# Two attention phases of a decoder run as one, over keys and queries that the projection has already split

## The reference

```python
s = einsum('bqhmd,bkhmd->bhmqk', qs, ks) * 64 ** -0.5    # two score maps
s = s + bias(q_pos - k_pos)[h]                           # constant from a distance of 128 on
s = where(q_pos >= k_pos, s, min)
p = softmax(s)
a = p[:, :, 0] - lam * p[:, :, 1]
out = einsum('bhqk,bkhd->bqhd', a, v)
```

## Time and profile before

| | |
|---|---|
| time, median of 3 runs | 3974.72 us (3974.5 to 3978.87) |
| the profiled execution's own time | 3976.59 us |
| its span | 3974.9 us |
| mean granted clock of PE | 0.951 |
| PE / DVE / ACT busy | 3534.9 / 1820.2 / 1157.0 us (89 / 46 / 29% of the span) |
| projections: vg, qka, qk, vg2 | 400, 230, 403, 406 us |
| prompt's attention, then samples' attention | 900, 263 us |

### The profile page before, as it was taken

The page is one execution under the profiler, slowest core; times in us unless marked ns, Lnnn a source line. Parts: engine busy times, 40 slices in busy tenths (PEclk is TensorE's granted clock), DMA queues, the critical chain, the costliest instruction groups (busy, mean ns, idle before and its releaser), DMA issues. The chain is left out here.

```text
span 3974.9 us, 56724 instructions
## 1 busy us (share of the span) xinstructions
PE 3534.9 (89%) x19647; PEld 2921.5 (73%) x19647; DVE 1820.2 (46%) x4012; ACT 1157.0 (29%) x1916; POOL 118.9 (3%) x157
## 2 busy tenths in 40 slices
PE   4999898996899989999999968888988867579999
PEld 3888797674688867887788857777777745468887
DVE  2222211555555532111322168888888822255554
ACT  2111111332221212100211146666666622221111
POOL 0000001110000000000000000000000000000000
PEclk9999998998899999999999979999999988789999
DMA  4211322335322213211412162222121066532221
GB/s 145 74 69 66 108 85 101 101 111 175 127 84 90 73 58 143 74 66 58 159 68 72 58 139 61 60 65 54 44 63 34 12 261 270 222 138 84 78 84 45
DMA packets 305099, 385.40 MB, mean 97 GB/s; under 512 B 153317, under 2 KB 211462, under 8 KB 304918
## 3 DMA queue, kind: packets, MB, share of 16 engines
q1 hardware_dynamic: 304918, 383.18, 29.1%
HBM read 278.63 MB, written 104.47 MB: 96 GB/s over the span
## 5 line engine op out<-in xcount | busy, mean ns | idle before, releaser
L234 PE MATMUL vg_ps_y<-vg_w_hi,vg_x_hi 128*128 128x512 f32 x1088 | 428.3, 394 | 11.1 <-DVE vg_w_lo L307 11.1
L236 PE MATMUL vg_ps_y<-vg_w_lo,vg_x_hi 128*128 128x512 f32 x1088 | 425.1, 391 | 0.0
L238 PE MATMUL vg_ps_y<-vg_w_hi,vg_x_lo 128*128 128x512 f32 x1088 | 425.0, 391 | 0.0
L1506 PE MATMUL att_ps_o<-att_v,att_a_t 128*128 128x128 f32 x2176 | 297.3, 285 | 51.6 <-ACT att_a_t L1567 51.2
L1506 PEld LDWEIGHTS att_ps_o<-att_v,att_a_t 128*128 128x128 f32 x2176 | 279.1, 198 | 76.4 <-ACT att_a_t L1567 53.4
L1634 DVE TENSOR_SCALAR_CACHE_REDUCE att_s<-att_ps_s,att_far 128x512 f32<-128x512 f32 (+3 forms) x608 | 326.5, 581 | 6.0 <-PE att_ps_s L1479 2.2
L1555 ACT ACTIVATE att_s<-att_s,att_neg 128x128 f32<-128x128 f32 (+15 forms) x256 | 307.2, 1200 | 2.3 <-DVE att_neg L1651 1.7
L1478 PE MATMUL att_ps_s<-att_k_hi,att_q_hl 128*128 128x512 f32 (+3 forms) x640 | 262.3, 416 | 11.7 <-DVE att_s L1634 10.8
L234 PEld LDWEIGHTS vg_ps_y<-vg_w_hi,vg_x_hi 128*128 128x128 f32 x1088 | 205.4, 189 | 54.1 <-issue 12.3
L1479 PE MATMUL att_ps_s<-att_k_lo,att_q_hl 128*128 128x512 f32 (+3 forms) x640 | 237.0, 375 | 0.0
L238 PEld LDWEIGHTS vg_ps_y<-vg_w_hi,vg_x_lo 128*128 128x128 f32 x1088 | 205.3, 189 | 42.9
(11 more groups left out here) (270 smaller groups left out, 6103.7 us busy)
## 6 DMA issues: line engine op xcount, KB each, us to landing
smp_k_pg<-in_cache_k SPq DMA_DIRECT2D x64, 512.0 KB, 5.7
smp_v_pg<-in_cache_v SPq DMA_DIRECT2D x64, 512.0 KB
factors<-vg_out SPq DMA_DIRECT2D x68, 256.0 KB, 2.0
res_factors<-factors SPq DMA_DIRECT2D x34, 512.0 KB
res_o<-mixer_out SPq DMA_DIRECT2D x34, 512.0 KB, 4.3
att_k_nat<-out_k SPq DMA_DIRECT2D x128, 128.0 KB, 2.6
att_q_nat<-diff_q SPq DMA_DIRECT2D x128, 128.0 KB, 3.0
gla_x<-gla_qka SPq DMA_DIRECT2D x17, 520.0 KB, 3.4
```

Source lines behind the costliest of these rows:

```text
L234: nc.tensor.matmul(ps_y[g][:, 0:width[g]], x_hi[u][:, k, :], w_hi[:, k, cols], start=(k == 0), stop=False)
L236: nc.tensor.matmul(ps_y[g][:, 0:width[g]], x_hi[u][:, k, :], w_lo[:, k, cols], start=False, stop=False)
L238: mm = nc.tensor.matmul(ps_y[g][:, 0:width[g]], x_lo[u][:, k, :], w_hi[:, k, cols], start=False, stop=(k == KD - 1))
L1506: mm = nc.tensor.matmul(ps_o[:, 0:D_VD], a_t[n % 2][:, (b % 4) * P:(b % 4 + 1) * P], v_sb[u][:, b, :], start=(b == 0), stop=(b == i))
```

## The change

**One projection phase per layer.** `project` now keeps the split x of all 17 tiles resident and streams the weights in pieces of 128 x 512 through a ring of nine, with the groups of columns outside and the tiles inside. It is called once per layer ("gla_in", 7 groups, and "diff_in", 8 groups). The four groups of queries and keys have the kind "turn": PE turns each prompt tile's result (4 transposes, `turn_out`), ACT makes the high part (with the factor 64 ** -0.5 for queries), DVE the low part, and SP stores both, already turned, in `qt`, `kh` and `kl` (5 transfers of 768 KB in all for a tile of queries, 2 of 512 KB for one of keys).

**One attention phase.** `attention` runs sample b beside head h = b. Keys and queries are loaded turned and split, so the `prep`s are gone. Scores go into two buffers of two banks (1024 columns) each: `cut` makes one entry of a tile with n up to 512 (both maps in one buffer), two up to 1024, four above (per map the left part and the right 1024). The low product contracts 64 rows (that map's half of the low keys) in place of 128. DVE takes an entry with one instruction: bias added and sign turned, with a running minimum, and no reduction or negation behind it. Within step g, PE does the first two entries of the scores of step g+2, then what `beside(g)` has of the sample (a key page's 8 transposes at the tiles i = 2 to 5 and 7 to 10; weights and values at i = 14, 15 and at i = 3 of the next head), and then the remaining entries between `turn` and `meet`. The sample's scores use one more entry of the same two buffers at two tiles of each head.

The diff, cut to its core:

```diff
 def project(...):
-        HALF = KD // 2
-        STAGES = 4
-        stage = [sb(f"stage{i}", [P, HALF, BANK]) for i in range(STAGES)]
...
+        x_hi = [sb(f"x_hi{t}", [P, KD, P], F32R) for t in range(TILES)]
+        x_lo = [sb(f"x_lo{t}", [P, KD, P], F32R) for t in range(TILES)]
+        w_hi = [sb(f"w_hi{r}", [P, BANK], F32R) for r in range(RING)]
+        w_lo = [sb(f"w_lo{r}", [P, BANK], F32R) for r in range(RING)]
+        stage = [sb(f"stage{i}", [P, BANK]) for i in range(STAGES)]
...
+                def turn_out(g, t):
+                    n, m = g * TILES + t, turned_before(g, t)
+                    pe.wait_ge(out_done[n % BANKS], after(n // BANKS + 1))
...
+                    for b in range(HB):
+                        mm = nc.tensor.transpose(ps_t[m % 2][:, b * P:(b + 1) * P],
+                                                 out[n % BANKS][:, b * P:(b + 1) * P], core.ident[:, :])
+                    mm.then_inc(s["out_turned"], 1)
...
 def attention(...):
+    def cut(n):
+
+        if n <= BANK:
+            return [[(m, 0, n, m * BANK, m) for m in range(2)]]
+        if n <= WIDE:
+            return [[(m, 0, n, 0, m)] for m in range(2)]
+        return [[(m, lo_, hi_, 0, m)] for m in range(2) for lo_, hi_ in ((0, n - WIDE), (n - WIDE, n))]
...
+                            for first, last, off in pieces:
+                                nc.tensor.matmul(dst[:, off:off + last - first], qs[:, m, :],
+                                                 k_hi[u][m][:, first:last], start=True, stop=False)
+                            half = slice(m * D_DH, (m + 1) * D_DH)
+                            for first, last, off in pieces:
+                                mm = nc.tensor.matmul(dst[:, off:off + last - first], qs[half, 2, :],
+                                                      k_lo[u][half, first:last], start=False, stop=True)
...
+                for g in range(STEPS):
+                    ahead = scores(g + 2) if g + 2 < STEPS else iter(())
+                    for _ in range(SLOTS):
+                        next(ahead, None)
+                    beside(g)
+                    mixed = values(g)
+                    for _ in ahead:
+                        next(mixed, None)
+                    for _ in mixed:
+                        pass
...
+                            nc.vector.tensor_tensor_reduce(
+                                out=sc[g % 2][:, m, lo_:hi_], in0=ps_s[(before + c) % SLOTS][:, off:off + w],
+                                in1=bias[h % 2][:, edge - w:edge], scale=-1.0,
+                                scalar=neg[g % 2][:, m, 0:1] if chained else 3.0e38, op0=ALU.add, op1=ALU.min,
+                                accum_out=neg[g % 2][:, m, side:side + 1]).then_inc(s["taken"], 1)
...
 def decoder(...):
-        project(core, "qka", x, w_gla[0], [
+        project(core, "gla_in", x, w_gla[0], halves(2 * GK, "copy", v)
+                + halves(2 * GK + GV, "silu", factors, g_gla[0]) + [
...
-        project(core, "qk", x1, w_diff[0], halves(0, "copy", q2) + halves(D, "copy", k_out))
+        project(core, "diff_in", x1, w_diff[0], halves(2 * D, "copy", v_out)
...
-        attention(core, q2, k_out, v_out, rev, rel_bias, o2)
-        core.end_phase()
-        sample_attention(core, q2, k_out, v_out, cache_k[0], cache_v[0], table, rev, rel_bias, o2)
+        attention(core, qt, kh, kl, q2, k_out, v_out, cache_k[0], cache_v[0], table, rev, rel_bias, o2)
```

More of the change, by code:

```diff
@@ L155, in project, with ps @@
[L155 to L161, removed]
+        def ps(name, n=BANK):
+            return mem.enter_context(nc.psum_tensor(f"{tag}_{name}", [P, n], F32))
@@ L219, in products @@
[L219 to L240, removed]
@@ new lines, in beside, with values @@
+                def beside(g):
+                    for what, n in step_turns(g)[0]:
+                        if what == "unit":
+                            turn_keys(n)
+                        elif what == "probs":
+                            probs(n)
+                        elif what in ("first", "second"):
+                            sample_values(n, int(what == "second"))
+                def values(g):
+                    count = groups[g % T]
+                    for c in range(count + 2):
+                        if c < count:
+                            turn(g, c)
+                        if c >= 2:
+                            meet(g, c - 2)
+                        if c >= 1:
+                            yield
@@ L1998, in _, with exps @@
-                output(B - 1)
+                def exps(g, m):
+                    n = (g % T + 1) * P
+                    maps = [x[0] for e in entries[g % T] for x in e]
+                    last = max(c for c, which in enumerate(maps) if which == m)
+                    pieces = maps.count(m)
+                    act.wait_ge(s["taken"], after(taken_before[g] + last + 1))
+                    if g >= 2:
+                        act.wait_ge(s["weight_done"], after(g - 1))
+                    nc.scalar.activation(sc[g % 2][:, m, 0:n], sc[g % 2][:, m, 0:n], ACT.Exp, scale=-1.0,
+                                         bias=neg[g % 2][:, m, pieces - 1:pieces],
+                                         accum_out=total[g % 2][:, m:m + 1]).then_inc(s["exp_done"], 1)
@@ new lines, in keys, with beside @@
+                def keys(n):
+                    unit_waits(act, n)
+                    dst, src = unit_keys(n)
+                    nc.scalar.activation(dst, src[:, :], ACT.Copy).then_inc(s["keys_even"], 1)
+                def beside(g):
+                    for what, n in step_turns(g)[0]:
+                        if what in ("probs", "probs_new", "first"):
+                            sample_back(n, what)
+                        elif what == "unit" and n % 2 == 0:
+                            keys(n)
@@ new lines, in sample_out @@
+                def sample_out(b):
+                    t = at_turn["second", b]
+                    dve.wait_ge(s["turned"], after(t + 1))
+                    dve.wait_ge(s["out_first"], after(b + 1))
+                    nc.vector.tensor_tensor(os_sb[:, :], ps_t[t % TURNS][:, 0:PAIR * D_VD], os_sb[:, :],
+                                            ALU.add).then_inc(s["out_second"], 1)
+                take(0)
+                for g in range(STEPS):
+                    h, i = divmod(g, T)
+                    if g + 1 < STEPS:
+                        take(g + 1)
+                    combine(g)
+                    for what, n in step_turns(g)[0]:
+                        if what == "unit" and n % 2 == 1:
+                            keys(n)
+                    if g == 3:
+                        place()
+                    if i == PROBS_AT - 1:
+                        sample_combine(h)
+                    if i == SECOND_AT - T and h >= 1:
+                        sample_out(h - 1)
```

1513 lines of the change are left out of this document (789 added, 724 removed).

## The result

The changed kernel takes 3922.64 us (median of 4 runs, 3919.78 to 3928.42) against 3975.55 for the one before in the same comparison: ratio 0.9869, 95% interval 0.9854 to 0.9885. It is faster, as forecast, but by 53 us and not by 182, and lies above the stated range. Its profiled span is 3921.4 us.

The account below looks back on a forecast made before the run. It took PE to bound the projections by their products, and the attention by PE's work in written order, not DVE or DMA. Profiled span 3974.9 - 30 + 4 - 156 = 3793 us; range 3660 to 3895.

Parts of the forecast that it names:

- The projections: Layer one's phase 600 us against 400 + 230, -30; layer two's 813 against 403 + 406, +4.
- 27 + 13: Layer two's projection: 27 us for 64 x 4 transposes of turned outputs, 13 for their interruptions of the products.
- the stores: Layer two's query tiles: 3.0 us of stores each under 5.4 of products, costed at nothing; 96 in all if uncovered.
- the price of a change of rows: Attention, per head: 96 changes between 128 and 64 rows at .10 us, half hidden by waits, 4.8 us.
- A second term: Attention, per head: DVE's work, 41 to 57 us plus 20 and 8, stays under 90, so charged nothing.
- The sum that went with it: Attention: tail of .16 us per change, 15.4 a head, 131.7 for 121.1, 85 more in all, some 3878.
- Rival B: Attention's long steps: written order makes a longer chain, 9.3 us more a head, 130.4, total 3867; chance .20.
- Rival C: Attention: row changes at full .35 us, 33.6 a head, 149.9 a head, total 4023; chance .06.
- Rival A: Attention: sample's work fills PE's gaps, changes cost .10 each, 107.2 us a head, total 3682; chance .22.
- 18.7 us of gaps: The earlier kernel's last head: 93.9 us less 75.2 at full pace; changes between kinds of work and short waits.
- the base of 116.3: Attention, one head before row changes: 93.9 us of the earlier last head plus 22.4 of the sample's PE work.
- The start: Attention's start, 24 us: 10 for page and bias transfers, 13 for keys and queries; 36 in the earlier kernel.

Follow-up runs that it names:

- the run with 128 rows: Changed kernel with the low product of the prompt's scores contracting 128 rows, the second map's query parts stored in swapped halves: 3797.03 us, ratio 0.9537.
- both flaws out: Changed kernel with the 128-row low product and DVE's key copy moved behind its first two takes: 3744.8 us, ratio 0.9411.
- the fastest version: Changed kernel with 128-row low product, later key copy, last value pages issued singly, third query part dropped, sample's second products at tile 6: 3708.99 us, ratio 0.9329.

## Why the prediction missed

**Right, nearly.** The projections: layer one's stretch is 610 us for 600 forecast, layer two's 820 for 813. From its first to its last work on PE layer one's takes 595 to 600 us in the nine experiments that have it, 602 in the changed kernel's profile, for 395 + 218 in that of before. For layer two's turned outputs 27 + 13 were forecast and 36 measured; the stores, costed at nothing, showed some 5. DMA's share of .43 in the attention was no bound.

**The step that failed** is the price of a change of rows, "so I take 96 x .10 / 2 = 4.8", in the paragraph on one head. It has two errors. The .10 came from a change of columns; a change of rows measures .2. It lies on both sides of the change: the last product ahead of it takes some .33 for .23, and the first one behind it as much, so that each pair of one shape takes .66 in the step above. The trace shows a part of the reason. In the changed kernel the weight load of the first low product starts only with that product, at 2917.24. In the run with 128 rows it starts .23 ahead of its product, which comes at 2959.81, beside the one that runs. The weight loads (PEld) of the changed kernel, and then of that run, are:

```profile
2917.24 0.29 PEld L1811 LDWEIGHTS att_ps_s<-att_k_lo,att_q 64*128 64x128 f32 x2 [0.36 <-issue]
```

```profile
2959.58 0.42 PEld L1810 LDWEIGHTS att_ps_s<-att_k_lo,att_q 128*128 128x128 f32 x2
```

Why the product ahead of a change is longer, too, stays open. And the half was a guess that waits would take up the rest; the run with 128 rows gives back 15.7 of the 19.7 a head. That is 11 to 15 us a head, 87 to 119 in all, of the 129 that the forecast is off.

**A second term**, put at nothing, failed beside it: "DVE isn't the bound, and I charge it nothing". DVE isn't the busiest, but PE waits for its take behind the key copy, and the order of these two alone costs 84 us. With both flaws out, 3744.8 us are measured, where the forecast without its 4.8 a head would be 3793 - 38 = 3755. So the two account for the miss, to within 10 us.

By the rule that I weighed in that place (the Trainium skill, "TensorEngine Tiling (Array Packing)", section Tiling Modes (Key Properties)) a change of the tiling mode drains TensorE. The .2 in two kernels agrees with a price for each such change; that it is a drain, no run shows. The sum that went with it, .16 x 96 = 15.4 a head, was much nearer than the one from the row of the recurrence; that it all but meets the 15.7 is chance, since a change costs .2 and waits take some of it back. I kept it out of the forecast for want of a row.

**Rival B** had the right place, a page's turning, DVE's key copy ahead of its take, and a third entry that waits, and 84 us is its price alone, near the 74 that it was given. The size is partly luck: 46 of the 84 are the wait, and some of the rest is clock, which B didn't count. I gave it .20, and priced it without the dear row change: the drain that I said I leave in its sum is not in its 130.4 a head. Together they would have been 3793 + 85 + 74 = 3952, above the 3922.64 measured; the range's end, 3895, had only a part of the changes. The chain was there in the written order, and the rows had all its durations. What stood against it, "there is time to catch up", is false with two buffers: DVE stood still for 2.07 us in the same step.

**Rival C** put the change of rows at .35, and the phase was to eat what the projections give from .29 on; it measured .2. **Rival A** was wrong: its 107.2 has 9.6 for the changes, so that 97.6 would be left without them. With both flaws out a head takes 113.2 us (outputs from 2312.0 to 3210.7), and 109 in the fastest version, which has three edits more. So of the 18.7 us of gaps the sample's work fills some 3 to 7, and the base of 116.3 was nearly right.

The sum a head: 113.2 with both flaws out, 15.7 for the rows, 10.5 for the chain (84 / 8), - 4 for what the two share (32 / 8), makes 135.4, against the 135.1 measured. The start was 10 longer than forecast (33.9 for 24); how much of that is PE's wait for the low keys (13.9 us), its wait for the sample's rows (15.4) or the barrier, no run separates.

## What to carry to other kernels

When a product is cut to fewer rows, count the changes of shape, not the work that it saves: the half-height product saved nothing here and cost 126 us. Where two streams share a written order, compare the orders of both engines item by item; a copy that waits for the other stream belongs behind the takes that are ready, and moving it on one engine changes what is best on the other. And a cost found in a kernel with slack is no price: the first 80 changes of rows a head cost 33 us, the next 80 159.

## What the runs showed of the hardware

A change between 128 and 64 contracted rows cost .2 us on TensorE, in two kernels, about the time of a whole 512-column product at .227. That a wait can cost twice was unexpected, too: behind one such wait in the changed kernel the products run slower for 10 us. PE's timeline there, and the granted clock of the two windows behind it (third value from the right):

```profile
3063.70 0.90 PE L1807 MATMUL att_ps_s<-att_k_hi,att_q 128*128 128x384 f32 x2 [1.52 <-DVE att_neg L2095]
3065.36 1.97 PE L1916 MATMUL att_ps_t<-ident,att_a 128*128 128x128 f32 x8
```

```profile
3065.00:3070.00 5.00, 5.00 (x18) 3.37 (x18) 1.55 (x5) 2.75 (x4) 0.00 (x0) 0.50 0.18 56
3070.00:3075.00 5.00, 5.00 (x26) 4.75 (x26) 2.78 (x5) 1.01 (x3) 0.00 (x0) 0.61 0.00 0
```

Eight transposes take 1.97 us in place of the 1.09 above, and the clock of .50 is the lower level, 1.2 of 2.4 GHz, to which PE fell behind the wait; within the second window it rose again. That one step took 15.4 us in place of 10.8. Not every wait of about that length was followed by it: in the step shown first the clock stayed up (1.00 from 2920 to 2923), and no run here tells the two apart. Over the attention the clock was .93 in the changed kernel and .97 in the fastest version.
